# Turning the chunk inverses of a gated delta rule by whole-array transposes, in a two-block transformer kernel on one core

## The chip, the cores and the metric

The kernel runs on one core of a Trainium2 chip. The time is the device time in microseconds of one execution of the program; the median of three runs stands for the kernel before.

## The reference

Two transformer blocks over 512 tokens of width 1024, all in float32. The first has a gated delta rule on eight heads beside sliding-window attention on eight heads, then a feed-forward part; the second has four mixers and a gated sum. The change touches only the triangular solve of the gated delta rule: for each of 8 heads and 8 chunks of 64 tokens, a unit lower triangular 64x64 matrix L is applied inversely to 128 columns.

```python
# first_block, gated delta rule (8 heads of 64, 8 chunks of 64 tokens)
decay = jnp.exp(jnp.where(causal, G[..., :, None] - G[..., None, :], -jnp.inf))
kb = k * beta[..., None]
A = jnp.where(strict, jnp.einsum('bhncd,bhnsd->bhncs', kb, k) * decay, 0.0)
L = A + jnp.eye(CHUNK, dtype=A.dtype)
rhs = jnp.concatenate([v * beta[..., None], kb * jnp.exp(G)[..., None]], axis=-1)
sol = lax.linalg.triangular_solve(L, rhs, left_side=True, lower=True, unit_diagonal=True)
u, w = sol[..., :Dv], sol[..., Dv:]
...
def step(S, inp):
    u_c, w_c, qk_c, qd_c, kd_c, dec_c = inp
    v_new = u_c - jnp.einsum('bhcd,bhde->bhce', w_c, S)
    o = jnp.einsum('bhcd,bhde->bhce', qd_c, S) + jnp.einsum('bhcs,bhse->bhce', qk_c, v_new)
    S = S * dec_c[..., None, None] + jnp.einsum('bhcd,bhce->bhde', kd_c, v_new)
    return S, o
...
# first_block around it
h = rms_norm(x, norm1_w[l]) * (1.0 + scale1) + shift1
proj = h @ w_in[l]                       # delta rule on 8 heads, window attention on 8 heads
mixed = jnp.concatenate([o_g, o_s], axis=-1) @ w_out[l]
x = x + gate1 * mixed
ffn = (jax.nn.silu(h2 @ w_gate[l]) * (h2 @ w_up[l])) @ w_down[l]
x = x + gate2 * ffn
# second_block: 16 meta tokens, four mixers (pooling, latent attention, conformer, short convolution), gates, w_o
```

## The kernel before

**Layout.** Two heads share a tile: head pair j (0 to 3) has one head on partitions 0 to 63 and the other on 64 to 127, and the eight chunks n lie side by side in 512 columns. `inv[j]`, `gE[j]`, `gW[j]`, `gA[j]`, `a32[j]` are such tiles of 128x512. A product of one head and one chunk is a 64x64 by 64x64 matmul, which uses one quarter of the PE array. A float32 matmul stands as two MATMUL records in the trace, a transpose as one, and each record of PE has a weight load (PEld) beside it.

**How L is inverted.** The diagonal 16x16 blocks are inverted by a short product series (stages d2, d4, d8, p1, p2, p3), which leaves the block-diagonal inverse in `inv[j]`. Two merges follow, the first from 16 to 32, the second from 32 to 64. A merge has three steps for each pair j: t turns `inv[j]` (each 64x64 block is transposed), z multiplies the blocks of L below the diagonal (`a32` for the first merge, `gA` for the second) with `inv[j]`, and c multiplies the turned inverse with z. DVE subtracts c from `inv[j]`. Keys are `t16`, `z16`, `c32` for the first merge and `t32`, `z32`, `c64` for the second. ACT copies t into `gW[j]` and z of the even pairs into `gE[j]`, DVE copies z of the odd pairs (`v.tensor_copy` at L2303), and `gather` (L2267) is the subtraction. `crossed_products` (L828 to L837, the matmul at L834) issues the products of two pairs together: those of the second pair write to the other half of the output partitions, so that all four quarters of the PE array are used in turn.

**After the merges.** `sol` applies `inv[j]` to both right sides (L911 to L913), `mq` multiplies the attention-like matrix with them (L925 to L927), DVE subtracts the results (L2316 and L2317), and the recurrence over the chunks follows.

**What sets the order.** Each engine has its own instruction stream, written by hand in one order; engines wait for one another on semaphores. PSUM has eight banks of 128x512, taken in turn by `open_tile`, which waits until the bank's last reader has passed. Weights come in panels of 128x2048 through three ring buffers (SP issues their DMAs), and each panel is split into a rounded part (`split_hi`, ACT, L1485) and a remainder (`split_lo`, DVE, L2004). Two such splits lie within the merges, those of the panels `out0` and `out1`, which PE needs first at L988, in the output projection. SP sends the loads of `out2` and what is behind it only once `sol` of the last pair has been filled.

**Names in the rows.** `arena` holds `inv`, `gE`, `gW` and `gA` in part; `inv[0]` is in `tb`, `inv[1]` in `acc`, `inv[2]` and `inv[3]` in `arena`. L825 is the matmul of `product`, which every other 64x64 product uses. L784 (window attention) and L976 are transposes over the whole array. L1657 is ACT's `move`.

Of the kernel before, what the change touches and what calls it, by code (L numbers as in the profile page):

```python
# [11 lines left out]
ALU = mybir.AluOpType  # L12
# [3 lines left out]
P = 128  # L16
# [101 lines left out]
def program(nc, a, out, known):  # L118
# [3 lines left out]
    with ctx:  # L122
# [171 lines left out]
        spare = [G1.take(T) for _ in range(2)]  # L294
        kdq = [G2.take(2 * T).rearrange("p (t c) -> p t c", t=2) for _ in range(NJ)]
# [276 lines left out]
        def _(pe):  # L572
# [255 lines left out]
            def crossed_products(name, j, left, right):  # L828

                o = [open_tile(pe, name, j + i) for i in range(2)]  # L830
                for n in range(NC):
                    for i in range(2):
                        for r, across in zip(both_heads, both_heads[::-1]):
                            last = mm(o[i][across if i else r, n * CH:(n + 1) * CH], left[i][r, n, :], right[i](n)[r],  # L834
                                      start=True, stop=True)
                        if n == NC - 1:
                            last.then_inc(*fill(name, j + i))  # L837
# [53 lines left out]
            for size, block, stage in ((16, a32, "a32"), (32, gA, "a64")):  # L891
                before = "p3" if size == 16 else "c32"
                for j in (0, 2):
                    for i in (j, j + 1):
                        pe.wait_ge(*copied(before, i))
                    crossed_products(f"t{size}", j, inv[j:j + 2], [lambda n: eye] * 2)
                    for i in (j, j + 1):
                        pe.wait_ge(*done(stage, i))
                    crossed_products(f"z{size}", j, block[j:j + 2], [lambda n: inv[j][:, n, :], lambda n: inv[j + 1][:, n, :]])
                for j in (0, 2):  # L900
                    for i in (j, j + 1):
                        pe.wait_ge(*copied(f"t{size}", i))
                        pe.wait_ge(*copied(f"z{size}", i))
                    crossed_products(f"c{2 * size}", j, gW[j:j + 2], [lambda n: gE[j][:, n, :], lambda n: gE[j + 1][:, n, :]])
            for j in range(NJ):
                pe.wait_ge(*copied("c64", j))
                pe.wait_ge(*copied("kt", j))
                pe.wait_ge(*copied("vt", j))
                sides = pairs_of(qkv[:, 4 + j:9 + j:4, :])
                for half in range(2):  # L910
                    o = open_tile(pe, "sol", j, half)  # L911
                    product(o, inv[j], lambda n: sides[:, n], range(4 * half, 4 * half + 4), P)\
                        .then_inc(*fill("sol", j, half))  # L913
# [430 lines left out]
        def _(pool):  # L1344
# [70 lines left out]
            for j in range(NJ):  # L1415
                pool.wait_ge(*filled("z32", j))
                pool.wait_ge(*done("eglast", j))
                times(gA[j], chunked("eye"), eglast[j].unsqueeze(2).broadcast_to([P, NC, CH])).then_inc(*signal("eg", j))
# [30 lines left out]
        def _(act):  # L1449
# [235 lines left out]
            for size in (16, 32):  # L1685
                for j in (0, 2):
                    move(f"t{size}", j, gW[j])
                    move(f"t{size}", j + 1, gW[j + 1])
                    move(f"z{size}", j, gE[j])
# [293 lines left out]
        def _(dve):  # L1983
# [316 lines left out]
            for size, before in ((16, "p3"), (32, "c32")):  # L2300
                for j in (1, 3):
                    dve.wait_ge(*filled(f"z{size}", j))
                    v.tensor_copy(gE[j], whole(f"z{size}", j)).then_inc(*read(f"z{size}", j))  # L2303
                for j in range(NJ):
                    dve.wait_ge(*copied(before, j))
                    gather(f"c{2 * size}", j, ALU.subtract)
                split_lo()
# [418 lines left out]
```

## Time and profile before

| What | Value |
|---|---|
| median of 3 runs | 1280.85 us (1279.19 to 1282.63) |
| the profiled execution's own time | 1281.56 us |
| its span, first to last instruction | 1279.6 us |
| PE busy | 1224.3 us, 96% of the span |
| DVE busy | 702.1 us, 55% |
| ACT busy | 492.0 us, 38% |
| the merges (285.0 to 308.3 us of the span) | 23.3 us, PE busy 13.85 us |

The profiled time is 0.71 us above the median, and 1.96 us of it lie outside the span. PE is busy nearly all the time; the merges are a short stretch in which it isn't. In the views below, "issue" is idle time in which an engine waited for nothing that the profile shows, and a record's time is modelled, since matmuls overlap: what counts is how far the starts are apart.

### The profile page before, as it was taken

To read this page: it belongs to the slowest core of one execution; us is meant where nothing else is said; L and a number is where in the kernel's file an instruction comes from. 1 tells how busy PE (TensorE), PEld (TensorE's weight loads), DVE (VectorE), ACT (ScalarE), POOL (GpSimd) and SP (SyncE) were. 2 spreads that over 40 slices of the span, in tenths; PEclk is the share of its full clock that TensorE was granted. 3 is DMA by queue.
4 is the path that set the end of the run, shared out by engine and by line. 5 is a ranking of instruction groups with operands and counts; after the bars stand their busy time and mean duration, and the time that the engine had idled before them with its cause. 6 is when DMAs were issued, how large, how long until landed. Compare 5 with 4: busy or idle time off the path is not lost.

```text
span 1279.6 us, 20461 instructions
## 1 busy us (share of the span) xinstructions
PE 1224.3 (96%) x8672; PEld 998.0 (78%) x8672; DVE 702.1 (55%) x1018; ACT 492.0 (38%) x774; POOL 104.6 (8%) x151
## 2 busy tenths in 40 slices
PE   2899999997998999999999999999999999999998
PEld 2577778786887888888888889798767678888886
DVE  4699878654467535322332457858465646334344
ACT  4443543664245422211222334223446654222232
POOL 4000004621020000000000110000002320000000
PEclk9899999999998999999999999999999999999999
DMA  9666611001222444234322243323231115433311
GB/s 309 223 202 189 219 58 36 3 4 36 68 66 66 134 130 148 75 107 132 99 87 62 83 132 109 99 63 94 50 79 46 34 38 136 116 90 87 106 47 66
DMA packets 150954, 125.62 MB, mean 98 GB/s; under 512 B 16984, under 2 KB 134513, under 8 KB 150736
## 3 DMA queue, kind: packets, MB, share of 16 engines
q1 hardware_dynamic: 147888, 119.88, 31.0%
q10 hardware_dynamic: 1744, 2.36, 0.5%
q0 software_dynamic: 1232, 2.07, 0.5%
q8 instruction: 69, 1.13, 0.4%
q14 instruction: 21, 0.17, 0.0%
HBM read 122.20 MB, written 2.10 MB: 97 GB/s over the span
## 4 chain that ended last, share of the span: by engine, by line
PE 89%; DVE 4%; DMA 2%; ACT 2%; issue 1%; POOL 0%; ACTq 0%; DVEq 0%; POOLq 0%
PE bank L583 55%; PE bank L676 5%; PE bank L825 5%; PE bank L1255 4%; PE bank L1226 3%; PE bank L1289 3%; PE bank L1143 2%; DMA arena<-in_meta_tokens_dram 1%; PE bank L988 1%; PE bank L1117 1%; PE bank L834 1%; PE bank L1176 1%; PE bank L1198 1%; PE bank L1156 1%; DVE wlo L2004 1%
## 5 line engine op out<-in xcount | busy, mean ns | idle before, releaser
L583 PE MATMUL bank<-hsplit,whi 128*128 128x512 f32 (+1 forms) x1872 | 552.5, 379 | 0.8 <-DVE wlo L2004 0.7
L583 PEld LDWEIGHTS bank<-hsplit,whi 128*128 128x128 f32 x1872 | 341.7, 188 | 72.6 <-issue 8.0
L583 PE MATMUL bank<-hsplit,wlo 128*128 128x512 f32 (+1 forms) x936 | 352.7, 377 | 0.0
L2004 DVE TENSOR_TENSOR wlo<-ring,whi 128x2048 fp32r<-128x2048 f32 (+4 forms) x97 | 196.9, 2030 | 178.5 <-ACT whi L1485 178.2
L1485 ACT ACTIVATE whi<-ring 128x2048 fp32r<-128x2048 f32 (+4 forms) x97 | 165.4, 1705 | 127.0 <-DVE xT L2354 53.3
L583 PEld LDWEIGHTS bank<-hsplit,wlo 128*128 128x128 f32 x936 | 176.2, 188 | 32.7
L583 PE MATMUL bank<-a_split,whi 128*128 128x512 f32 x340 | 104.8, 390 | 0.0
L583 PEld LDWEIGHTS bank<-a_split,whi 128*128 128x128 f32 x340 | 63.9, 188 | 13.1
L583 PE MATMUL bank<-a_split,wlo 128*128 128x512 f32 x170 | 66.2, 390 | 0.0
L2033 DVE SCALAR_TENSOR_TENSOR post<-ring,small,post 128x512 f32<-128x512 f32 x77 | 57.9, 752 | 3.1 <-DMA ring<-in_w_ada_dram 0.4
L1426 POOL TENSOR_TENSOR acc<-acc,tb 128x512 f32<-128x512 f32 x12 | 15.5, 1294 | 435.3 <-ACT tb L1723 435.3
L1489 ACT ACTIVATE a_split<-tb 128x512 fp32r<-128x512 f32 x22 | 13.8, 632 | 88.1 <-DVE tb L2398 87.9
L2354 DVE SCALAR_TENSOR_TENSOR xT<-bank,small,xT 128x512 f32<-128x512 f32 x24 | 17.9, 748 | 50.5 <-PE bank L583 40.1
L1226 PE MATMUL bank<-hsplit,whi 128*128 128x512 f32 x128 | 44.3, 427 | 0.0
L1255 PE MATMUL bank<-arena_r,whi 128*128 128x512 f32 x136 | 42.1, 391 | 0.2 <-issue 0.2
L2398 DVE TENSOR_TENSOR tb<-bank,tb 128x512 f32<-128x512 f32 x22 | 14.9, 690 | 48.1 <-PE bank L583 46.6
L2466 DVE SCALAR_TENSOR_TENSOR arena<-arena,V 128x512 f32<-128x512 f32 x60 | 40.3, 746 | 0.0
L1289 PE MATMUL bank<-whi,m_split 128*128 128x512 f32 x128 | 39.8, 390 | 0.0
L676 PE MATMUL bank<-hsplit,whi 128*128 128x512 f32 (+1 forms) x128 | 33.8, 357 | 4.9 <-DVE hsplit L2009 3.9
L1748 ACT ACTIVATE tb<-bank 128x512 f32<-128x512 f32 x20 | 12.0, 599 | 68.2 <-PE bank L583 68.2
L583 PEld LDWEIGHTS bank<-a_split,wlo 128*128 128x128 f32 x170 | 31.9, 188 | 6.6
L1255 PEld LDWEIGHTS bank<-arena_r,whi 128*128 128x128 f32 x136 | 25.5, 188 | 5.9 <-issue 0.6
(443 smaller groups left out, 1731.7 us busy)
## 6 DMA issues: line engine op xcount, KB each, us to landing
ring<-in_w_ada_dram SPq DMA_DIRECT2D x24, 1024.0 KB, 5.3
ring<-in_w_in_dram SPq DMA_DIRECT2D x22, 1024.0 KB, 5.2
ring<-in_w_in_dram SPq DMA_DIRECT2D x34, 512.0 KB, 5.2
ring<-in_w_gate_dram SPq DMA_DIRECT2D x11, 1024.0 KB, 5.3
ring<-in_w_up_dram SPq DMA_DIRECT2D x11, 1024.0 KB, 5.3
ring<-in_w_down_dram SPq DMA_DIRECT2D x8, 768.0 KB, 4.8
ring<-in_w_down_dram SPq DMA_DIRECT2D x8, 640.0 KB, 4.3
ring<-in_w_out_dram SPq DMA_DIRECT2D x4, 1024.0 KB, 5.3
```

Of the source, the lines that this page charges most:

```text
L583: last = mm(o[0:m, 0:n], w[:, k, c0:c0 + m], rhs(s, k), start=k + i == 0, stop=k == kn - 1 and i == 2)
L676: last = mm(o[:, 0:n], w[:, k, c0:c0 + P], rhs(s, k), start=at + i == 0, stop=at == len(order) - 1 and i == 2)
L825: last = mm(o[r, i * width:(i + 1) * width], left[r, n, :], right(n)[r], start=start, stop=stop)
L1143: mm(o[:, 0:m0], q_mla[:, h, i * WIN:(i + 1) * WIN], k_mla[:, h, 0:m0], start=True, stop=True)\
L1226: last = mm(early[0][:, :], w[:, k, P * (b % 2):P * (b % 2) + P], hx(s, k), start=k + x == 0, stop=k == KD - 1 and x == 2)
L1255: last = mm(o[:, :], w[:, k0 + k, c0:c0 + P], y[kb + k], start=k + i == 0, stop=k == nk - 1 and i == 2)
L1289: last = mm(fo[b][:, :], mix_split[:, s, 4 * kp + k, b * P:(b + 1) * P], w[:, k, :], start=kp + k + i == 0, stop=kp == 1 and k == 3 and i ...
L1485: split_hi = splitter(act, lambda hi, src: A(hi, src, ACT.Copy), None)
L2004: split_lo = splitter(dve, None, lambda lo, src, hi: tt(lo, src, hi, ALU.subtract))
L2033: last = stt(out=acc, in0=w[:, k, :], scalar=c, in1=acc, op0=ALU.mult, op1=ALU.add)
L2354: stt(out=xT[:, m, :], in0=bank(*key)[:, :], scalar=modT[:, gate + m:gate + m + 1], in1=xT[:, m, :], op0=ALU.mult, op1=ALU.add).then_inc(* ...
L2466: stt(out=conf_sum[:, m, :], in0=src, scalar=tap, in1=conf_sum[:, m, :], op0=ALU.mult, op1=ALU.add))
```

## The change

In both merges the inverse is no longer turned by 64x64 products with an identity, but by four transposes over the whole array for each pair of heads, each on a 128x128 block that holds two chunks of two heads. That also swaps what lies on the partitions: the turned inverse has the chunk's parity there (even chunks on 0 to 63, odd ones on 64 to 127) and the head in the columns. So z is written in the same layout (`heads_to_chunks`: one bank for each head, the parity on the partitions), and c takes both from there and writes back to head rows (`chunks_to_heads`: one bank for each parity). ACT copies the bank of head 0 of z, DVE that of head 1, each for two pairs. DVE's subtraction now takes one parity of one pair at a time, so it comes in eight pieces of 128x256 in place of four of 128x512 in each merge. POOL and the next products wait for both banks of a pair of pairs. Both `split_lo` of DVE stand behind the second merge.

```diff
--- before.py
+++ after.py
@@ -292,6 +292,8 @@
         t2_all, ta_all = (G1.take(NJ * T).rearrange("p (j t) -> p j t", j=NJ) for _ in range(2))
         gE, gW, gA = ([by_chunk(t[:, j, :]) for j in range(NJ)] for t in (t1_all, t2_all, ta_all))
         spare = [G1.take(T) for _ in range(2)]
+        z_of_head = t1_all.rearrange("p j (b h c) -> p h j b c", b=NB, h=2)
+        bank_by_pair = lambda t: t.rearrange("p (j b c) -> p j b c", j=2, b=NB)
         kdq = [G2.take(2 * T).rearrange("p (t c) -> p t c", t=2) for _ in range(NJ)]
         dd = [G2.take(2 * T).rearrange("p (t c) -> p t c", t=2) for _ in range(NJ)]
         a32_flat = [spare[0], spare[1], post[:, 0:T], post[:, T:2 * T]]
@@ -825,16 +827,29 @@
                         last = mm(o[r, i * width:(i + 1) * width], left[r, n, :], right(n)[r], start=start, stop=stop)
                 return last
 
-            def crossed_products(name, j, left, right):
-
-                o = [open_tile(pe, name, j + i) for i in range(2)]
-                for n in range(NC):
-                    for i in range(2):
-                        for r, across in zip(both_heads, both_heads[::-1]):
-                            last = mm(o[i][across if i else r, n * CH:(n + 1) * CH], left[i][r, n, :], right[i](n)[r],
-                                      start=True, stop=True)
-                        if n == NC - 1:
-                            last.then_inc(*fill(name, j + i))
+            all_quarters = ((0, 0), (1, 1), (0, 1), (1, 0))
+
+            def heads_to_chunks(name, j, left, right):
+
+                o = [open_tile(pe, name, j, h) for h in range(2)]
+                for i, b in product_order:
+                    for h, q in all_quarters:
+                        r, n, c = both_heads[h], 2 * b + q, (4 * i + b) * CH
+                        last = mm(o[h][both_heads[q], c:c + CH], left[j + i][r, n, :], right[j + i][r, n, :], start=True, stop=True)
+                        if (i, b) == product_order[-1] and (h, q) in all_quarters[2:]:
+                            last.then_inc(*fill(name, j, h))
+
+            def chunks_to_heads(name, j, left, right):
+
+                o = [open_tile(pe, name, j, q) for q in range(2)]
+                for i, b in product_order:
+                    for q, h in all_quarters:
+                        r, n, c = both_heads[q], 2 * b + h, (4 * i + b) * CH
+                        last = mm(o[q][both_heads[h], c:c + CH], left[j + i][r, n, :], right[j + i][r, n, :], start=True, stop=True)
+                        if (i, b) == product_order[-1] and (q, h) in all_quarters[2:]:
+                            last.then_inc(*fill(name, j, q))
+
+            product_order = [(i, b) for i in range(2) for b in range(NB)]
 
             def tile_product(name, j, left, right):
 
@@ -889,21 +904,29 @@
                 tile_product("p3", j, second[j], inv[j])
                 window(4 * NJ + 1 + j)
             for size, block, stage in ((16, a32, "a32"), (32, gA, "a64")):
-                before = "p3" if size == 16 else "c32"
                 for j in (0, 2):
                     for i in (j, j + 1):
-                        pe.wait_ge(*copied(before, i))
-                    crossed_products(f"t{size}", j, inv[j:j + 2], [lambda n: eye] * 2)
+                        if size == 16:
+                            pe.wait_ge(*copied("p3", i))
+                        elif i == j:
+                            pe.wait_ge(*copied("c32", j, 0))
+                            pe.wait_ge(*copied("c32", j, 1))
+                        o = open_tile(pe, f"t{size}", i)
+                        for b in range(NB):
+                            last = tr(o[:, b * P:(b + 1) * P], inv_flat[i][:, b * P:(b + 1) * P], ident)
+                        last.then_inc(*fill(f"t{size}", i))
                     for i in (j, j + 1):
                         pe.wait_ge(*done(stage, i))
-                    crossed_products(f"z{size}", j, block[j:j + 2], [lambda n: inv[j][:, n, :], lambda n: inv[j + 1][:, n, :]])
+                    heads_to_chunks(f"z{size}", j, block, inv)
                 for j in (0, 2):
                     for i in (j, j + 1):
                         pe.wait_ge(*copied(f"t{size}", i))
-                        pe.wait_ge(*copied(f"z{size}", i))
-                    crossed_products(f"c{2 * size}", j, gW[j:j + 2], [lambda n: gE[j][:, n, :], lambda n: gE[j + 1][:, n, :]])
+                    for h in range(2):
+                        pe.wait_ge(*copied(f"z{size}", j, h))
+                    chunks_to_heads(f"c{2 * size}", j, gW, gE)
             for j in range(NJ):
-                pe.wait_ge(*copied("c64", j))
+                for q in range(2):
+                    pe.wait_ge(*copied("c64", j - j % 2, q))
                 pe.wait_ge(*copied("kt", j))
                 pe.wait_ge(*copied("vt", j))
                 sides = pairs_of(qkv[:, 4 + j:9 + j:4, :])
@@ -1413,7 +1436,8 @@
             for point in range(2 * NJ + 1, 5 * NJ + 1):
                 window(point)
             for j in range(NJ):
-                pool.wait_ge(*filled("z32", j))
+                for h in range(2):
+                    pool.wait_ge(*filled("z32", j - j % 2, h))
                 pool.wait_ge(*done("eglast", j))
                 times(gA[j], chunked("eye"), eglast[j].unsqueeze(2).broadcast_to([P, NC, CH])).then_inc(*signal("eg", j))
 
@@ -1686,7 +1710,8 @@
                 for j in (0, 2):
                     move(f"t{size}", j, gW[j])
                     move(f"t{size}", j + 1, gW[j + 1])
-                    move(f"z{size}", j, gE[j])
+                    act.wait_ge(*filled(f"z{size}", j, 0))
+                    A(z_of_head[:, 0, j:j + 2], bank_by_pair(bank(f"z{size}", j, 0)[:, :]), ACT.Copy).then_inc(*read(f"z{size}", j, 0))
                 split_hi()
             for j in range(NJ):
                 for half in range(2):
@@ -2297,14 +2322,24 @@
                 dve.wait_ge(*copied("p2", j))
                 gather("p3", j)
                 window(4 * NJ + 1 + j)
-            for size, before in ((16, "p3"), (32, "c32")):
-                for j in (1, 3):
-                    dve.wait_ge(*filled(f"z{size}", j))
-                    v.tensor_copy(gE[j], whole(f"z{size}", j)).then_inc(*read(f"z{size}", j))
-                for j in range(NJ):
-                    dve.wait_ge(*copied(before, j))
-                    gather(f"c{2 * size}", j, ALU.subtract)
-                split_lo()
+            for size in (16, 32):
+                for j in (0, 2):
+                    dve.wait_ge(*filled(f"z{size}", j, 1))
+                    v.tensor_copy(z_of_head[:, 1, j:j + 2], bank_by_pair(bank(f"z{size}", j, 1)[:, :]))\
+                        .then_inc(*read(f"z{size}", j, 1))
+                for j in (0, 2):
+                    for q in range(2):
+                        if size == 32:
+                            dve.wait_ge(*copied("c32", j, q))
+                        dve.wait_ge(*filled(f"c{2 * size}", j, q))
+                        for i in range(2):
+                            if size == 16:
+                                dve.wait_ge(*copied("p3", j + i))
+                            blocks = inv[j + i][:, q::2, :]
+                            tt(blocks, blocks, bank_by_pair(bank(f"c{2 * size}", j, q)[:, :])[:, i], ALU.subtract)\
+                                .then_inc(*(read(f"c{2 * size}", j, q) if i else signal("part")))
+            split_lo()
+            split_lo()
             for j in range(NJ):
                 q_j = by_chunk(qkv[:, j, :])
                 dve.wait_ge(*done("eg", j))
```

**PE, start of the first merge.** The last product of the series, then t16 and z16 of pairs 0 and 1. Before:

```order
L825 MATMUL bank1<-arena,hscratch 64x64 x15
L834 MATMUL bank2<-consts,tb 64x64 [waits bank2_read,bank3_read,bank6_read,bank4_read]
L834 MATMUL bank2<-consts,tb 64x64
L834 MATMUL bank3<-consts,acc 64x64 x2
...
L834 MATMUL bank4<-tb,arena 64x64 [waits bank4_read,bank5_read,a32]
L834 MATMUL bank4<-tb,arena 64x64
L834 MATMUL bank5<-acc,arena 64x64 x2
```

After:

```order
L827 MATMUL bank1<-arena,hscratch 64x64 x15
L916 MATMUL bank2<-consts,tb 128x128 [waits bank2_read,bank4_read]
L916 MATMUL bank2<-consts,tb 128x128 x3
L916 MATMUL bank3<-consts,acc 128x128 [waits bank3_read,bank6_read]
L916 MATMUL bank3<-consts,acc 128x128 x3
L838 MATMUL bank4<-tb,arena 64x64 [waits bank4_read,bank5_read,a32]
L838 MATMUL bank5<-tb,arena 64x64
L838 MATMUL bank4<-tb,arena 64x64
```

The 32 products of 64x64 against `consts` (the identity) have become eight transposes of 128x128; the products of z are as many as before, one bank for each head, and wait for the same signals. The same happens at the other three places where an inverse is turned.

**DVE, first merge.** Copies of z (COPY), subtractions (TENSOR_TENSOR with a bank), and the remainder of a panel (`wlo`). Before, from the copy of z16 of pair 1 on:

```order
L2303 COPY arena<-bank5 128x512 [waits bank5_filled]
L2303 COPY arena<-bank1 128x512 [waits bank1_filled]
L2267 TENSOR_TENSOR tb<-tb,bank2 128x512 [waits bank2_filled,bank4_read]
L2267 TENSOR_TENSOR acc<-acc,bank3 128x512 [waits bank3_filled,bank6_read]
L2267 TENSOR_TENSOR arena<-arena,bank4 128x512 [waits bank4_filled,bank0_read]
L2267 TENSOR_TENSOR arena<-arena,bank5 128x512 [waits bank5_filled,bank1_read]
L2004 TENSOR_TENSOR wlo0<-ring2,whi0 128x2048 [waits w_hi]
L2303 COPY arena<-bank1 128x512 [waits bank1_filled]
```

After, from the copy of z16 on:

```order
L2328 COPY arena<-bank5 128x8x64 [waits bank5_filled]
L2328 COPY arena<-bank1 128x8x64 [waits bank1_filled]
L2339 TENSOR_TENSOR tb<-tb,bank2 128x4x64 [waits bank4_read,bank2_filled]
L2339 TENSOR_TENSOR acc<-acc,bank2 128x4x64 [waits bank6_read]
L2339 TENSOR_TENSOR tb<-tb,bank3 128x4x64 [waits bank4_read,bank3_filled]
L2339 TENSOR_TENSOR acc<-acc,bank3 128x4x64 [waits bank6_read]
L2339 TENSOR_TENSOR arena<-arena,bank4 128x4x64 [waits bank0_read,bank4_filled]
L2339 TENSOR_TENSOR arena<-arena,bank4 128x4x64 [waits bank1_read]
L2339 TENSOR_TENSOR arena<-arena,bank5 128x4x64 [waits bank0_read,bank5_filled]
L2339 TENSOR_TENSOR arena<-arena,bank5 128x4x64 [waits bank1_read]
L2328 COPY arena<-bank1 128x8x64 [waits bank1_filled]
L2328 COPY arena<-bank5 128x8x64 [waits bank5_filled]
```

Four subtractions of 128x512 have become eight of 4x64 columns, two from each bank, and the panel's remainder has moved away from between the merges.

**DVE, end of the second merge.** Before, from the subtraction for pair 2 on:

```order
L2267 TENSOR_TENSOR arena<-arena,bank0 128x512 [waits bank0_filled,bank4_read]
L2267 TENSOR_TENSOR arena<-arena,bank1 128x512 [waits bank1_filled,bank5_read]
L2004 TENSOR_TENSOR wlo1<-ring0,whi1 128x2048 [waits w_hi]
L2316 TENSOR_TENSOR arena<-arena,bank2 128x256 [waits bank2_filled,qe,eg]
L2317 TENSOR_TENSOR arena<-arena,bank2 128x256
```

After, from the second piece for pairs 2 and 3 on:

```order
L2339 TENSOR_TENSOR arena<-arena,bank0 128x4x64
L2339 TENSOR_TENSOR arena<-arena,bank1 128x4x64 [waits bank1_filled,bank5_read]
L2339 TENSOR_TENSOR arena<-arena,bank1 128x4x64
L2029 TENSOR_TENSOR wlo0<-ring2,whi0 128x2048 [waits w_hi]
L2029 TENSOR_TENSOR wlo1<-ring0,whi1 128x2048 [waits w_hi]
L2351 TENSOR_TENSOR arena<-arena,bank2 128x256 [waits bank2_filled,qe,eg]
L2352 TENSOR_TENSOR arena<-arena,bank2 128x256
```

Both remainders now stand in a row between the last subtraction of the merges and the first subtraction after `mq`.

## Rows read from the trace of the kernel before

**Rows 1.** The page, busy time and DMA queues.
```profile
PE 1224.3 (96%) x8672; PEld 998.0 (78%) x8672; DVE 702.1 (55%) x1018; ACT 492.0 (38%) x774; POOL 104.6 (8%) x151
...
q8 instruction: 69, 1.13, 0.4%
```

**Rows 2.** The page, chain that ended last, by line.
```profile
PE bank L583 55%; PE bank L676 5%; PE bank L825 5%; PE bank L1255 4%; PE bank L1226 3%; PE bank L1289 3%; PE bank L1143 2%; DMA arena<-in_meta_tokens_dram 1%; PE bank L988 1%; PE bank L1117 1%; PE bank L834 1%; PE bank L1176 1%; PE bank L1198 1%; PE bank L1156 1%; DVE wlo L2004 1%
```

**Rows 3.** Stretches: engines' busy us (instructions), clock, DMA.
```profile
262.00:285.00 23.00, 23.00 (x491) 18.79 (x492) 12.51 (x30) 15.20 (x37) 6.23 (x6) 1.00 0.01 3
285.00:308.30 23.30, 13.85 (x778) 12.91 (x776) 9.42 (x12) 10.72 (x16) 4.13 (x4) 1.00 0.02 5
308.30:316.00 7.70, 7.70 (x144) 7.70 (x144) 3.49 (x3) 4.70 (x9) 0.00 (x0) 1.00 0.02 4
316.00:341.00 25.00, 23.61 (x590) 22.80 (x586) 11.39 (x27) 6.42 (x13) 0.00 (x0) 1.00 0.40 128
```

**Rows 4.** PE's waits, 285 to 308.3: us, times, longest.
```profile
PE bank L834 <- issue: 9.4, 7, 1.9
```

**Rows 5.** Chain of waits, 284 to 310: start us, us, what.
```profile
285.22 2.07 PE bank L834 x132
287.29 1.51 issue
288.79 2.22 PE bank L834 x123
291.01 1.59 issue
292.60 2.18 PE bank L834 x124
...
306.38 1.62 issue
308.00 0.34 PE bank L834 x5
308.33 1.72 PE bank L825 x29
```

**Rows 6.** DMA, 280 to 312: GB/s in 40 slices of 0.8 us; packets.
```profile
GB/s 0 0 0 0 0 0 0 31 0 0 0 0 20 0 0 0 0 20 0 0 0 20 0 0 0 0 20 0 0 0 0 20 0 0 0 0 20 0 0 0
...
q8 instruction: 7, 0.11, 1.6%
```

**Rows 7.** Chain, 262 to 350: whole-array turns, densest later products.
```profile
279.05 0.59 PE bank L784 x4
...
329.72 3.02 PE bank L825 x96
...
347.93 1.75 PE bank L976 x16
```

**Rows 8.** DVE in time, 280 to 332: start us, us, what.
```profile
290.88 0.69 DVE L2303 COPY arena<-bank 128x512 f32<-128x512 f32 x1 [2.93 <-PE bank L834]
293.78 0.69 DVE L2267 TENSOR_TENSOR tb<-tb,bank 128x512 f32<-128x512 f32 x1 [2.21 <-PE bank L834]
...
294.98 1.27 DVE L2267 TENSOR_TENSOR arena<-arena,bank 128x512 f32<-128x512 f32 x2
296.18 2.28 DVE L2004 TENSOR_TENSOR wlo<-ring,whi 128x2048 fp32r<-128x2048 f32 x1
...
309.52 2.28 DVE L2004 TENSOR_TENSOR wlo<-ring,whi 128x2048 fp32r<-128x2048 f32 x1
316.45 0.42 DVE L2316 TENSOR_TENSOR arena<-arena,bank 128x256 f32<-128x256 f32 x1 [4.64 <-PE bank L825]
```

**Rows 9.** ACT in time, 280 to 312.
```profile
289.88 1.57 ACT L1657 ACTIVATE arena<-bank 128x512 f32<-128x512 f32 x3 [2.09 <-PE bank L834]
291.32 1.92 ACT L1485 ACTIVATE whi<-ring 128x2048 fp32r<-128x2048 f32 x1
```

**Rows 10.** One line, DVE half-width subtraction: ns min/median/max.
```profile
L2316 DVE TENSOR_TENSOR arena<-arena,bank x8: 420/422/422, 316.4 to 325.3; 128x256 f32<-128x256 f32 x8
```

## The prediction

> **What bounds the kernel now.** I read the page first: PE is busy for 1224.3 of 1279.6 us [rows 1], and the chain of waits runs over PE almost everywhere; L834, the line that the change replaces, holds 1% of it [rows 2]. So the change can move only its own stretch, and what it saves there reaches the end only if PE is the last one there and behind it. The table by stretches shows where the merges differ from their surroundings: from 262 to 285 and from 308.3 to 316 PE is busy throughout, from 285 to 308.3 for 13.85 of 23.3 us, at full clock and with DVE busy for only 9.42 us [rows 3]. The list of PE's waits puts 9.4 us of that on "issue", in seven pieces [rows 4]: no engine that the profile shows released them. The chain in order of time shows their rhythm: about 130 records in 2.1 to 2.2 us, a stop of 1.4 to 1.9 us, and so on [rows 5]. The stops fall inside runs of products whose semaphores were passed at the run's start: the first stands six products into t16 of pairs 2 and 3 (2 x 64 records for t16 and z16 of the first two pairs, and six more). A data wait can't do that.
>
> The DMA view names the cause. Weights are silent there, and the little that moves is seven packets of instruction code in 32 us, in slices 7 to 36 of 0.8 us, thus one every (36 - 7) x 0.8 / 6 = 3.9 us [rows 6]. The page has 69 such packets and 1.13 MB for the run [rows 1], so 16.4 KB each, and 8672 matmul records and as many weight loads over 69 are 251 instructions a packet, or some 126 matmul records. That is the distance between the stops. PE resumed at 288.79 and 292.60, and at 308.00 after five such blocks [rows 5]: (308.00 - 288.79) / 5 = 3.84 us a block. A packet starts about 1 us after PE has entered a block, and PE enters the next one 2.8 us later: one block is fetched ahead and no more. Products that use four quarters in turn pass at 2.07 us / 132 = 16 ns a record [rows 5], 2 us a block, so they outrun the fetch. Just before and behind, 126 records take over 5 us (491 in 23 us, 144 in 7.7 us, 590 in 25 us [rows 3]), and nothing stops.
>
> The Trainium skill ("Advanced Engine Details and Errata", ISA Cache) gives a cache line as 16 KB or 256 instructions, in which the trace agrees (251 and a few waits a packet). It also gives TensorE 128 KB but says there are only two lines: with eight lines the fetch would have run ahead during the 20 us before, and the 768 records would hardly have stopped. The stop after 134 records decides for two.
>
> **The change part by part.**
>
> *Records of PE.* A merge stage before is 2 merges x (t, z, c) x 4 pairs x 16 products x 2 records = 768. The products of t go (256 records); 32 transposes come, one record each as in L784 and L976 [rows 7]. That leaves 544, and z and c keep their number, their four quarters and their 16 to 17 ns. Time of the turns: 8 transposes for 64 records. Those of L784, which stand between products, take 0.59 us for four on the chain, 0.148 each; those of L976, in a row, 1.75 us for 16, 0.109 each [rows 7]. So 0.9 to 1.2 us for eight in place of 1.05 us: no gain and no loss of its own. I take 0.95, nearer to the row of many in a row.
>
> The Trainium skill ("TensorEngine Tiling (Array Packing)", Key Properties) says that changing the tiling mode drains the array, which speaks against this change: it adds eight changes. The two rows of transposes differ by 0.04 us each, or 0.16 us for a group of four between products, and four groups of eight would cost 0.6 us by it if they were on the path. They aren't wherever PE arrives at a code block early.
>
> *Code blocks.* Six stops lie before: after about 134, 260, 385, 511, 637 and 763 of the 768 records. The boundaries after the change lie at the same distances, since everything before the merges is the same: 134, 260, 386 and 512 of 544. Four are left. The packet for the first is triggered when PE's sequencer enters the block before the merges, so it comes at the same time, and the resumes stay where they were: 288.8, 292.6, 296.4 and 300.3 us.
>
> *Does the data keep up?* I follow it with rows of before. t16 ends at 285.95, z16 at 287.0, t16 of pairs 2 and 3 at 287.95, z16 at about 289.0. ACT needs 0.5 to 0.6 us a copy (three in 1.57 [rows 9]), DVE 0.69 [rows 8]; both copies of z16 are there at 289.9. c32 of the first two pairs runs from 289.1, of the others from about 290.1, and stops at record 260: 1.5 us of waiting for code, until 292.6, and ends at 292.8. The eight subtractions of 128x256: the nearest row is L2316, 0.42 us from a bank [rows 10]; four make about 1.6 us where two of 128x512 made 1.27 [rows 8]. Those of pairs 0 and 1 are done while PE waits for code, those of 2 and 3 at about 294.6. t32 and z32 of pairs 0 and 1 cover them until 294.85. t32 of 2 and 3 ends at 295.8, z32 reaches its boundary (record 386) at 296.4, just when the code is there, and ends at 296.9. c64 of the first pairs follows, that of the others starts at 297.95 behind DVE's copy (297.8) and meets record 512 at 298.5. It waits until 300.3, and its last 32 records take 0.55: the merges end at 300.85, where they ended at 308.33 [rows 5]. That is 7.5 us less. The one boundary without slack is the third; I allow 0.3 us for it and take **7.2 us**.
>
> *Bounds.* For DVE's pieces: if both strided sides cost nothing, the stage can't beat the code, so 7.5 stays; if they cost as much as a full 0.69 us, a pair of pairs takes 2.8 instead of 1.6 us, the third boundary slips by about 1.0 us, and the gain is 6.3. ACT's strided copies: the rows give 0.50 to 0.6 for any 128x512 copy; nothing to change.
>
> *The panel remainders on DVE.* The one at 296.18 lay between the merges and ended at 298.46, before its successor was wanted; it cost nothing on PE's path, since the code came later. Now both stand behind the merges: the last subtractions end at about 301.05 + 1.6 = 302.65, and two remainders of 2.28 us [rows 8] end at 307.1. Behind them wait the subtractions of mq. The first ran at 316.45 after 4.64 us of idleness [rows 8], 8.1 us after sol began at 308.33; with sol from 300.85 it is wanted at 309.0. So 1.9 us of that cover are left, and a later DVE would cost what exceeds it. ACT's two rounded parts (1.92 us [rows 9]) keep their places, the second now at about 298 to 300. The loads of out2, out3 and the first gate panel wait for sol of the last pair and move forward with it; out0 and out1 are wanted at 341, so nothing there is late.
>
> *Behind the merges.* POOL's four products (4.13 us [rows 3]) start when z32 is full, at about 295, and are done before 300; they are wanted at 309. The densest later products pass at 3.02 us / 96 = 31 ns a record [rows 7], 3.96 us a block, just over the 3.84 us of a fetch. Moving the boundaries by 224 records can cost a few tenths at the worst. From there on PE is the chain, and the gain reaches the end.
>
> **The sum.** 1281.56 us (the profiled execution) - 7.2 = 1274.4 us. The profiled one lies 0.7 us above the median of the runs shown, 1280.85; I predict the median: 1280.85 - 7.2 = **1273.7 us**. Its own range is 1272 to 1276.
>
> **The rivals.**
>
> *The data chain ends last (gain 3 to 6).* A third boundary that is missed by 2 us or more, because transposes drain the array at 0.25 us each, or because the pieces on DVE take 0.7 to 0.9 us and the remainders then end after 309. For it: the slack at that boundary is nil. Against it: 1.5 and 1.8 us of slack at the boundaries on either side. The time would be about 1276.5 us.
>
> *The stops aren't code (gain none).* If each hand-over of banks costs PE its 1.5 us whatever lies between, the six stops stay, the turns cost the same, and DVE has 8 instructions more, under 1 us: 1280.5 to 1281.5 us, no difference. For it: the profile names no releaser, and some blocks of 126 records happen to end near the start of a run of 64. Against it: the packets' rhythm, and stops in the middle of runs.
>
> *DVE becomes the bound (slower).* The new subtraction reads and writes runs of 64 columns with gaps in both SBUF and the bank, a form that no row of before shows. With x us for one of the 16 pieces, DVE's path from 290.3 is about 2.9 + 16x us long; before, sol of pair 2 began near 311.8. It decides from x = (311.8 - 293.2) / 16 = 1.16 us. At 1.4 us the merges end 3.8 us later than before, and the two remainders come behind them: about 1285 us. Against it: L2316 reads a bank with such gaps in 0.42 us [rows 10], and only a form nearly three times as dear would do it.
>
> **How the numbers follow.** Forecast 0.76; data chain 0.10; none 0.09; slower 0.05. A change of this kernel's time under 0.3%, 3.8 us, can't be told from none. Faster by more than that: the forecast and most of the second case, 0.84; within: 0.11; slower: 0.05. The range of 8 in 10 goes from 1271.5 (a gain of 7.5 and the spread of the three runs, 1.7 us below their median) to 1277.8, which takes in the data chain down to a gain of 3.
>
> **What the profile of the changed kernel would show.** Right: PE's "issue" idleness in the merges falls from 9.4 to about 4 us, in four or five pieces of which one is near zero; sol begins near 301; the stretch to it has some 544 records; packets of code still come every 3.8 to 3.9 us, one or two fewer over the run (67 or 68). DVE's pieces take 0.35 to 0.42 us, and its first subtraction of mq still waits for PE, for 1 to 2 us. Wrong: pieces above 0.7 us, PE waiting for DVE's subtractions by name, or stops of 1.5 us at every run in spite of fewer records. If the packets come further apart than 3.9 us, the forecast fails at the fetch; if the transposes take over 0.2 us each, at the turns.

## The result and the profile after

The changed kernel takes 1274.52 us (median of 6 runs, 1272.7 to 1275.15) against 1281.82 us for the kernel before (6 runs, 1279.19 to 1282.63): a ratio of 0.9946, 95% interval 0.9934 to 0.9958, or 7.3 us less. The forecast was 7.2 us less, 1273.7 us; that the time itself came out 0.8 us higher is the base, whose median is 1281.82 us over six runs and was 1280.85 over the first three. Its profiled execution took 1274.51 us with a span of 1272.6 us, against 1281.56 and 1279.6.

First the page of the changed kernel: busy times, and the queue that brings code. They answer to [rows 1].

```profile
PE 1223.9 (96%) x8448; PEld 995.4 (78%) x8448; DVE 701.9 (55%) x1026; ACT 492.4 (39%) x774; POOL 104.9 (8%) x151
...
q8 instruction: 67, 1.10, 0.4%
```

PE has 224 records fewer and is as busy as before; two packets of code fewer came. The table by stretches, whose columns are those of [rows 3], with the merges now from 285 to 301:

```profile
285.00:301.00 16.00, 13.24 (x528) 11.76 (x524) 7.70 (x17) 11.32 (x17) 4.10 (x4) 1.00 0.02 5
301.00:309.00 8.00, 8.00 (x174) 8.00 (x175) 5.82 (x6) 4.47 (x8) 0.00 (x0) 1.00 0.01 4
```

PE is busy for 13.24 of 16.0 us where it was for 13.85 of 23.3. PE's work hardly shrank, the gaps between did. The chain of waits of the changed kernel in order of time (start us, us, what) answers to [rows 5]; L916 are the transposes, L838 the products of z, L848 those of c, L827 those of sol:

```profile
285.44 1.02 PE bank L916 x8
286.46 1.09 PE bank L838 x64
...
290.81 1.00 PE bank L848 x50
291.81 0.83 issue
292.64 0.46 PE bank L848 x11
...
296.24 1.23 PE bank L838 x64
...
298.61 0.68 PE bank L848 x28
299.30 1.66 issue
300.95 0.74 PE bank L848 x32
301.69 10.31 PE bank L827 x203
```

The reader is to count records here. Between 286.46 and 290.81 lie another group of 8, one of 64 and the first 64 of c, so 8 + 64 + 8 + 64 + 64 + 50 = 258 pass before the first real stop, of 0.83 us. The second, of 1.66 us, stands 28 records into the last c64, before which the program has 480, so at 508 (a trace lacks a few records, and counts are good to about five). Near record 384 a run of z takes 1.23 us in place of 1.09. No stop at 133: PE came there at about 289.5, after the code. sol begins at 301.69 where it began at 308.33. From the run's first record to sol it is 16.25 us (301.69 - 285.44) and was 23.11 (308.33 - 285.22), 6.86 less; the merges began 0.22 us later, so sol begins 6.64 us earlier. From there to the end of the span it is 970.9 us, and it was 971.3: nothing was given back. The packets of code, in 40 slices of 0.4 us from 286 to 302:

```profile
GB/s 41 20 0 0 0 0 0 0 0 41 0 0 0 0 0 0 0 0 0 0 41 0 0 0 0 0 0 0 0 0 41 0 0 0 0 0 0 0 0 0
```

The last three start in slices 9, 20 and 30, counted from 0, so (30 - 9) x 0.4 / 2 = 4.2 us apart.

DVE in order of time, which answers to [rows 8], and one line of the transposes (ns min/median/max):

```profile
290.76 0.42 DVE L2339 TENSOR_TENSOR tb<-tb,bank 128x256 f32<-128x256 f32 x1 [0.31 <-PE bank L848]
...
293.13 1.42 DVE L2339 TENSOR_TENSOR arena<-arena,bank 128x256 f32<-128x256 f32 x4 [0.95 <-PE bank L848]
...
303.13 4.49 DVE L2029 TENSOR_TENSOR wlo<-ring,whi 128x2048 fp32r<-128x2048 f32 x2
309.68 0.42 DVE L2351 TENSOR_TENSOR arena<-arena,bank 128x256 f32<-128x256 f32 x1 [2.06 <-PE bank L827]
```

```profile
L916 PE MATMUL bank<-consts,arena x16: 272/272/328, 287.5 to 296.0; 128*128 128x128 f32 x16
```

A transpose's record is 272 ns long, but eight pass in 1.02 us, 0.128 each, since records overlap. A piece of the new subtraction takes 0.42 us and four of them 1.42 us. The copy of z32, at 295.31, waits for PE. Both remainders lie in 303.13 to 307.6, and after them DVE waits 2.06 us for PE.

### The profile page after: what moved, and what is told of

Read it like the earlier page. It is cut to its first block, busy times and chain, and to the rows that moved or that the text cites. A ratio compares the mean times of both kernels' runs of the same rounds, so it can differ in the third digit from the quotient of the medians.

```text
span 1272.6 us, 20019 instructions
## 1 busy us (share of the span) xinstructions
PE 1223.9 (96%) x8448; PEld 995.4 (78%) x8448; DVE 701.9 (55%) x1026; ACT 492.4 (39%) x774; POOL 104.9 (8%) x151
## 4 chain that ended last, share of the span: by engine, by line
PE 88%; DVE 5%; ACT 3%; DMA 3%; issue 1%; POOL 0%; ACTq 0%; DVEq 0%; POOLq 0%
PE bank L585 54%; PE bank L827 5%; PE bank L678 4%; PE bank L1278 4%; PE bank L1249 4%; PE bank L1312 3%; PE bank L1166 2%; DMA arena<-in_meta_tokens_dram 1%; PE bank L1011 1%; PE bank L1140 1%; DVE wlo L2029 1%; PE bank L1199 1%; DMA ring<-in_w_in_dram 1%; PE bank L1221 1%; PE bank L1179 1%
## 5 line engine op out<-in xcount | busy, mean ns | idle before, releaser
L1450 POOL TENSOR_TENSOR acc<-acc,tb 128x512 f32<-128x512 f32 x12 | 15.5, 1294 | 433.8 <-ACT tb L1748 433.8
```

## The experiments

The theory, called code below: PE waits in the merges for the next 256 instructions, of which one block is fetched ahead. Its rivals: the new layout and DVE's order made the gain; each hand-over between runs has a price of its own; the position of the code is of no account. Where the length of the merges is given, it runs from their first record to sol: 23.1 us before, 16.25 after. The medians and ratios are against the kernel before, measured with each on the same chip.

**e1: the turns by products again, all else as changed.**

```diff
-                        for b in range(NB):
-                            last = tr(o[:, b * P:(b + 1) * P], inv_flat[i][:, b * P:(b + 1) * P], ident)
+                    o = [open_tile(pe, f"t{size}", j + h) for h in range(2)]
+                    for i, b in product_order:
+                        for h, q in all_quarters:
+                            r, n, c = both_heads[h], 2 * b + q, (4 * i + b) * CH
+                            last = mm(o[h][both_heads[q], c:c + CH], inv[j + i][r, n, :], eye[r], start=True, stop=True)
...
```

The lines left out signal each bank; ACT's copies of t go by the bank of each head, as its copy of z does.

> The changed kernel, but the inverses are turned by 64x64 products with the identity again, written in the new layout (one bank for each head, chunk parity on the partitions). Layout, DVE pieces and the place of the two panel remainders are those of the change; only the number of PE records goes back from 544 to 768 in the merges, at the same PE time (64 records of 16 ns for 8 transposes of 0.128 us). Theory code (PE waits for the next 256 instructions, fetched one block ahead, about 3.9 us each): six stops again, sol begins near 308.5 us of the span, the whole gain is lost, 1281.5 us against 1274.5. Rival layout (what was gained comes from the new order of the data, the pieces on DVE or the moved remainders): stays at 1274.5. Rival hand-over (a stop of 1.5 us belongs to a change between runs of products): also 1274.5, since the runs are as many as in the changed kernel.

Measured: 1282.33 us (1280.43 to 1282.96), ratio 1.0003 (0.9994 to 1.0013). The whole gain is gone. The chain of waits of e1 (L919 the turns, L839 z, L849 c), its beginning and its end:

```profile
285.22 0.93 PE bank L919 x62
286.16 0.96 PE bank L839 x62
287.12 0.12 PE bank L919 x6
287.24 1.58 issue
...
306.53 1.62 issue
...
308.48 2.52 PE bank L828 x44
```

The products of the turn take 0.93 us for 62 records, less than the 1.02 us of the eight transposes; all the same the first stop stands at 62 + 62 + 6, some 130 records, the sixth ends at 308.14, and sol begins at 308.48 (308.5 expected). The layout, the pieces on DVE and the late remainders are all there and are worth nothing. This is the experiment that settles the question: the rivals layout and hand-over fall.

**e2: the changed kernel with the first remainder back between the merges.**

```diff
-            split_lo()
-            split_lo()
+                split_lo()
```

> The changed kernel with the first panel remainder (DVE, 2.28 us) back between the two merges. Theory code: it ends at about 296.9, so the copy of z32 moves from 295.3 to 296.9 and c64 begins about 0.1 to 0.3 us later at most, in front of a stop of 1.66 us that takes it up: sol near 301.7, no difference (within 0.3 us). Rival remainder (moving it was the gain, or a part): 2 to 4 us slower than the changed kernel, 1276.5 to 1278.5.

Measured: 1273.58 us (1272.59 to 1274.79), ratio 0.9941 (0.9925 to 0.9958), as the changed kernel. DVE and, behind it, the chain of waits:

```profile
293.92 2.28 DVE L2029 TENSOR_TENSOR wlo<-ring,whi 128x2048 fp32r<-128x2048 f32 x1
296.12 0.68 DVE L2328 COPY arena<-bank 128x512 f32<-128x512 f32 x1
```

```profile
298.89 1.66 issue
...
301.29 9.73 PE bank L827 x192
```

The copy of z32 can begin only as the remainder ends, at 296.12 (295.31 in the changed kernel), and PE idles 0.23 us ahead of c64; the code stop behind it still ends the stretch. sol begins at 301.29, 15.85 us after the merges' start. The total shows no loss.

**e3: the kernel before with both remainders behind the merges.**

```diff
-                split_lo()
+            split_lo()
+            split_lo()
```

> The kernel before with nothing changed but both panel remainders behind the merges. Theory code: no difference from the kernel before, sol at 308.3. Rival remainder: 2 to 4 us faster than before.

Measured: 1281.55 us (1279.91 to 1283.49), ratio 1.0002 (0.9993 to 1.0011): no difference. e2 and e3 together: this part of the change is free in both directions. Its profiled execution has one thing that was not expected, in the chain of waits:

```profile
284.58 2.07 PE bank L834 x132
...
287.61 2.21 PE bank L834 x123
...
305.45 0.34 PE bank L834 x5
305.78 5.25 PE bank L825 x94
```

The same stops after the same numbers of records, but PE resumed every (305.45 - 287.61) / 5 = 3.57 us, where the kernel before had 3.84 [rows 5], and the merges took 21.2 us in place of 23.1. That profiled run took 1279.91 us, the shortest of its ten. The edit can't shorten a stop inside a run of products; PE's instructions are the same, so a fetch took longer in one execution than in the other, and six of them add up to (3.84 - 3.57) x 6 = 1.6 of the 1.9 us. It is not the session: e1, measured beside e3, resumed every 3.87 us, (308.14 - 288.81) / 5. What sets it stays open.

**e4: the kernel before on half the array.**

```diff
-                        for r, across in zip(both_heads, both_heads[::-1]):
-                            last = mm(o[i][across if i else r, n * CH:(n + 1) * CH], left[i][r, n, :], right[i](n)[r],
+                        for r in both_heads:
+                            last = mm(o[i][r, n * CH:(n + 1) * CH], left[i][r, n, :], right[i](n)[r],
                                       start=True, stop=True)
```

> The kernel before, but the products of the merges use two quarters of the PE array in place of four: those of the second pair aren't crossed any more. As many records, 768, at about 31 ns each where they had 16. Theory code: 126 records now take 3.9 us, as long as a fetch, so the stops vanish and the merges last 24 us in place of 23.3: about 1 us slower than before, 1282.5, sol near 309.4, PE busy throughout. Rival hand-over: the stops of 9.4 us stay and 10 us of PE time come on top, 1291.

Measured: 1281.34 us (1278.76 to 1283.43), ratio 1.0001 (0.9991 to 1.001). The chain of waits:

```profile
286.66 11.25 PE bank L834 x385
297.92 0.15 issue
298.06 7.98 PE bank L834 x255
...
310.32 0.74 PE bank L825 x11
```

The records pass at 11.25 us / 385 = 29 ns in place of 16, and of the stops 0.3 us is left in three pieces. The merges last 23.7 us, 0.55 more than before; sol begins at 310.32 (309.4 expected), since they also began 1.4 us later. Doing the same work on half the array cost nothing that can be measured: the four quarters had only made PE wait. The forecast of 1 us more is below what the times can tell. The rival hand-over, 1291 us, falls.

**e5, e6 and e7: the same code, moved.**

```diff
             pe.wait_ge(*arrived("const"))
+            for _ in range(40):
+                mm(banks[7][:, 0:1], ident, ident[:, 0:1], start=True, stop=True)
             pe.wait_ge(*arrived("x", 2))
```

In e6 the loop runs 52 times; in e7 it stands in the kernel before.

> The changed kernel with 40 tiny products (128x1, 80 records of PE and as many weight loads, each writing one unused column of a bank) in the 20 us at the start in which PE waits for its first data. They cost nothing where they stand, but every later instruction lies 160 places further on, so in the merges the block boundaries fall at records 53, 178, 303 and 429 of 544 in place of 8, 133, 258, 384 and 509, and their packets are triggered earlier. Theory code, with 3.9 us a fetch (3.6 in a quicker execution): stops of 0.6, 0.5 and 0.9 us at 178, 303 and 429, sol begins near 300.3 (299.4) us where it began at 301.7: 1.2 to 1.6 us less, 1273 us. Any rival in which the position of the code is of no account: stops as in the changed kernel, 1.66 us inside the last c64, sol near 301.7.

> As e5, with 52 tiny products (104 records). The boundaries fall at records 153, 278, 404 and 529, the last one 15 records ahead of sol, so a fifth block must have come before sol can begin. Theory code: stops of 0.6, 0.7, 0.7 and 1.8 us, sol near 302.1 (300.9 with 3.6 us a fetch): 0.2 to 0.4 us later than the changed kernel and 1.5 to 1.8 later than e5. Rival: as e5's rival, sol near 301.7 with the stop of 1.66 us at record 508.

> The kernel before with the 80 records of e5. Boundaries at 53, 178, 303, 429, 554 and 680 of 768. Theory code: five stops of 1.1 to 1.8 us in place of six, none within the first 170 records, sol near 306.8 (305.3 with 3.6 us a fetch) where it began at 308.3: about 1.6 us less, 1280. Rival: as before, the first stop at record 134.

Measured: e5 1278.32 us (1276.29 to 1283.3), ratio 0.9982 (0.9971 to 0.9992), so slower than the changed kernel; e6 1285.62 us, ratio 1.003 (1.0017 to 1.0043); e7, on the kernel before, 1286.7 us, ratio 1.0036 (1.0023 to 1.0049). The totals missed what was expected, for a reason at the other end of the program. The filler of e5, by its line:

```profile
L642 PE MATMUL bank<-consts x80: 352/352/373, 10.9 to 27.8; 128*128 128x1 f32 x80
```

80 records between 10.9 and 28.1 us are 0.215 us each: a 128x128 float32 weight load each, for one column. They outlast the idle 20 us, everything starts later, and the merges begin at 288.59 in e5, 295.86 in e6 and 288.92 in e7 instead of 285.2 to 285.4. The filler is not all of it. Ahead of the merges PE waits for POOL (`wscratch`) for 2.1 us in the kernels before and after, at about 226, and in e6, at about 237; in e5, e7 and e8 this wait is 0.5 us. With the long wait the granted clock also fell to half of full speed for 3.4 us or more (0.50 from 238.9 to 242.3 in e6), and in e5, e7 and e8 it did not fall there. So e6 starts 7.3 us after e5, though its filler ends only 5.1 later. e7 loses another 2.4 us behind sol, which isn't traced.

Within the merges the theory can be read without that. The chains of e5, of e6 and of e7, the start of the merges, stops and sol:

```profile
288.59 1.02 PE bank L918 x8
...
297.04 0.14 issue
...
300.45 0.51 issue
...
302.95 0.58 issue
303.54 0.87 PE bank L829 x12
```

```profile
295.86 1.02 PE bank L918 x8
...
310.50 1.69 issue
...
312.63 5.39 PE bank L829 x98
```

```profile
288.92 2.81 PE bank L836 x181
291.73 1.37 issue
...
308.81 1.57 PE bank L836 x83
310.39 7.66 PE bank L827 x137
```

Counted as above, the stops stand where the addresses put them:

| Kernel | Boundaries expected, records | Stops found after record (us) |
|---|---|---|
| changed kernel, e2, e9 | 134, 260, 386, 512 | 258 (0.83, 0.29, 0.56), 508 (1.66, 1.66, 0.86) |
| e5 | 53, 178, 303, 429 | 305 (0.14), 430 (0.51) |
| e6 | 153, 278, 404, 529 | 156 (0.08), 408 (0.66), 533 (1.69) |
| e7 | 53, 178, 303, 429, 554, 680 | 181 (1.37), 306 (1.41), 429 (1.16), 555 (1.79), 680 (1.77) |

In e7 five stops are left of six, and sol begins 310.39 - 288.92 = 21.5 us after the merges' start in place of 23.1, 1.6 us less, as expected; a quicker fetch isn't the reason, for PE resumed every (308.81 - 293.10) / 4 = 3.93 us. In e6 it is 16.8 us against 16.25 in the changed kernel, 0.5 more (0.2 to 0.4 expected), with a stop of 1.69 us just before the end. In e5 it is 15.0 us, 1.3 less. The stops expected at 178 in e5 and at 278 in e6 are missing. What wasn't expected is that e5 and e6 idle 0.30 and 0.51 us at record 272, where the second merge begins: the profile names no releaser there, but in e8, which does the same, the turns start at 291.90, as the DVE subtraction before them ends (291.39 + 0.41). The places of the stops are what shows that the position of the code counts. The lengths show less: the changed kernel's own merges took 16.25 us in its profile, 15.85 in e2 and, below, 15.05 in e9, so the 15.0 of e5 is no proof of a gain.

**e8 and e9: a cheaper filler, and the changed kernel again beside it.**

```diff
             pe.wait_ge(*arrived("const"))
+            for _ in range(10):
+                for r, q in ((0, 0), (HD, HD), (0, HD), (HD, 0)):
+                    mm(banks[7 if r == q else 6][q:q + HD, 0:1], ident[r:r + HD, 0:HD], ident[r:r + HD, 0:1], start=True, stop=True)
             pe.wait_ge(*arrived("x", 2))
```

> The changed kernel with the same 80 records at the start as e5, but as 64x1 products on the four quarters of the array in turn. In e5 each record took 0.215 us there, 17.2 us in all from 10.9 us on, so the first transposes began at 28.1 in place of 20 us and the merges about 3 us later. If a quarter's record costs a quarter of that, 80 take about 4 us and are over before the first data arrive at about 20 us; the merges begin at 285.4 as in the changed kernel. Theory code: stops as in e5 (1.0 us together before the last subtractions), sol 14.7 to 15.0 us after the merges' start in place of 16.25, so near 300.3: 1.3 us less than the changed kernel, 0.10%, about 1273. Rival (a shift only moves the cost elsewhere): sol near 300.3, but the total as the changed kernel's or above.

> The changed kernel once more, on the same chip as e8, as the measure for it: 1274.5 us, 0.5 to 0.6% below the kernel before, sol near 301.5 with stops of 0.1 to 0.9 us near record 258 and of 1.5 to 1.8 us near 508.

Measured: e8 1273.55 us (1271.92 to 1275.46), ratio 0.9934 (0.9921 to 0.9948); e9, the changed kernel, 1274.31 us, ratio 0.994 (0.9928 to 0.9953). The chains of waits of e8 and of e9, start of the merges and their end:

```profile
285.06 1.02 PE bank L919 x8
...
293.51 0.68 issue
...
297.46 0.51 issue
...
299.96 0.58 issue
300.55 0.87 PE bank L830 x12
```

```profile
284.98 1.02 PE bank L916 x8
...
298.43 0.86 issue
...
300.03 17.98 PE bank L827 x393
```

Now the merges of e8 begin on time (285.06), helped by the shorter wait for POOL, 0.5 in place of 2.1 us. Its code stops stand after records 305 and 430, as in e5. The 0.58 us ahead of sol aren't code: the last subtraction that sol needs starts on DVE at 300.03 and takes 0.41, and in e5 and in e8 the list of waits names DVE's subtraction as what sol's weight load waited for. e8's merges take 15.5 us where the changed kernel's took 16.25 in its first profile and 15.05 in e9, whose last stop was 0.86 us in place of 1.66. The expected 1.3 us lie within what one execution differs from another, and the difference of the medians, 0.06%, is inside both intervals. (The profiled executions are no pair: 1275.46 us is the longest of e8's five, 1272.82 the shortest of e9's.) e8 beats the kernel before; whether it beats the changed one isn't settled.

## Why the prediction was right

**What bounds.** Code was named from the rhythm of the stops and of the packets. e1 (same work and layout, 768 records, gain zero) and e4 (half the array, hardly a stop, same time) show it, and e5 to e8 that the stops sit where the addresses put them, within five records.

**The sum.** The mechanism held. That 7.3 us met 7.2 to 0.1 us is in part luck. In the two profiles the merges gave 6.86 us, 0.22 was lost ahead of them and 0.4 came behind, which no term of the sum has; one execution's merges differ from another's by 1.2 us with the same code (16.25 and 15.05). Against the 7.2 us of the sum, sol came 6.6 us earlier in the changed kernel's profile and 8.3 us earlier in e9's (300.03).

**Records and turns.** 544 records, as counted. Eight transposes took 1.02 us where 0.95 was taken, 0.128 each, between the two rows that bounded it. The 0.02 us above the back-to-back row make 0.6 us over 32, the price that the rule of the Trainium skill ("TensorEngine Tiling (Array Packing)", Key Properties: a change of tiling mode drains the array) was given; that the draining is its cause is not tested.

**Code blocks.** Expected at 134, 260, 386 and 512; found at 258 and 508, with 0.14 us near 384 and none near 133. The resume at 292.6 came at 292.64; the stop ahead of it was 0.83 us in place of 1.5 because PE got there later, at 291.81, after a later start and longer turns. The 0.84 us by which sol came late (301.69 for 300.85) arise behind it. The rest of c32 took 0.46 us in place of 0.2 and each of two groups of turns 0.07 more, so PE went on at the third boundary at about 296.8 in place of 296.4. From there to the last resume, at 300.95, it took 4.1 us in place of 3.9, and the last records 0.74 in place of 0.55. 0.3 us had been allowed for. "Issue" idleness is 2.7 us, not 4. One sign that the prediction named for an error at the fetch did appear: the packets came 4.2 us apart in the merges, not 3.8 to 3.9. In e9 the two resumes are (299.29 - 291.91) / 2 = 3.7 us apart, so this too changes from one execution to the next; why isn't known.

**DVE.** Four pieces took 1.42 us (1.6 taken), 0.34 apart. The rival in which DVE is the bound needed 1.16 us a piece. The cover of mq was forecast at 1.9 us and is 2.06. The remainders cost nothing in either place, as e2 and e3 show.

**Data.** At the third boundary, where the prediction had no slack, PE stopped for 0.14 us, so the data and the code came nearly together. e5 and e8 show what comes next: with the code moved, sol waits 0.58 us for DVE, and the second merge's turns 0.30 us, it seems for DVE too. So these runs give no sign that much is left to be had from the code's position alone.

**One block ahead.** Blocks of 256 instructions, one of them fetched ahead, put the stops where they were found in every kernel here. In this the trace agrees with the Trainium skill ("Advanced Engine Details and Errata", ISA Cache), which gives a line of 256 instructions and two lines. It does not agree with the 128 KB for TensorE of the same section, if they are read as eight lines: by them the merges would have run through. That is worked out, not measured.

## What to carry to other kernels

When PE idles for "issue" inside a run of equal products, count its records from stop to stop and set that against the packets of the instruction queue: in this kernel a block of some 126 records took 3.6 to 3.9 us to come on the mean, so a stretch that passes well below about 30 ns a record (3.7 us / 126) ran at the speed of its code. There it pays to do the same work with fewer, larger instructions (a whole-array transpose for eight records of quarter products), and it pays nothing to make each one faster: the merges took 23.1 us at 16 ns a record and 23.7 at 29. Fill only with instructions whose own cost has been read from a row.

## What was not expected of the hardware

The time of a fetch differs between executions with the same instructions of PE: 3.84 us a block in the profile of before, 3.57 in e3's; and with one and the same kernel the last stop was 1.66 us in one profile and 0.86 in another. A 128x128 float32 weight load for a single column took 0.215 us a record at the start of the program, so 80 of them outlasted an idle of 9 us; as 64x1 products on the quarters the 80 took 2.3 us. Near 226 us the kernels before and after waited 2.1 us for POOL and had a stretch of 3.4 us or more with the granted clock at half; e5, e7 and e8 waited 0.5 us there and kept the full clock.
